# Encoder block with mixture of experts on one Trainium2 core: products moved in the tile loop, padding rows dropped from the scatter, the last expert unit taken out of the loop

## The chip, the cores and the metric

The kernel runs on one core of a Trainium2 (trn2) chip. The metric is the device time of one execution in microseconds (us). The time before is the median of 3 runs.

## What is computed

One layer over 2048 tokens of width 1024, in float32: a normalised and modulated input, a projection to q, k, v and u, windowed attention over chunks of 64 with sinks (8 query heads, 2 key heads), a pooling branch beside it, an output projection, and then a mixture of 128 experts with 8 chosen for each token, plus one shared expert.

```python
h = modulate(rmsnorm(x, norm1_g), shift1, scale1)
proj = h @ w_in                                   # q 512 | k 128 | v 128 | u 512
a = sink_window_attention(rope(q), rope(k), v, attn_sinks)
# pooling of u: band means over 2, 4, 8, 16 rows less u itself, then a 128x128 product per group
p = multiscale_pool(u, pool_w, pool_scale)
x = x + gate1 * (concat([a, p]) @ w_out)
h2 = modulate(rmsnorm(x, norm2_g), shift2, scale2)
# sigmoid router, 4 of 8 groups, 8 of 128 experts; each row of a chosen expert:
#   y = (silu(h2 @ w_gate[e]) * (h2 @ w_up[e])) @ w_down[e] * weight, added into its token's row
f = routed(h2) + swiglu(h2, w_sh_gate, w_sh_up, w_sh_down)
out = rmsnorm(x + gate2 * f, final_g)
```

2048 tokens times 8 experts are 16384 routed rows.

## The kernel before

**Order of the work.** Every engine has a queue written out by hand, with waits on named semaphores (`W8(engine, name, value)`; a wait stands in the code where the engine stops). No planner moves anything. The semaphores are named after who raises them: `p_` for TensorE, `v_` for VectorE, `a_` for ScalarE, and `B[0]` to `B[7]` are the eight PSUM banks.

**Tile loop.** The tokens go through in 16 tiles of 128 rows. `step(i)` runs on each engine for i from -2 to 17; in a step the engines work on tile i (attention and output projection), on tile i+1 (input projection), i+2 (norm), i-1 (second norm, router) and i-2 (ranks of the chosen experts, scatter of the records). On TensorE a step before the change is, in order: transposes of the next rows (L1148), scores (L1162), ranks (L1169, L1170), the input projection of the next tile (L1179, L1180, L1184), the band product of the pooling (L1191, L1192, into B[7]), transposes of h2 (L1148), transposes of the probabilities (L1200), the router product (L1211), the pool product (L1220, into B[1]), probabilities times values (L1225), transposes of the next q and k (L1233, L1234), and the output projection (L1246).

ScalarE copies PSUM banks: the projection's (L604, L605, L609, L610), the transposed h2 (L616, L617), v (L633 to L635); between them it takes the mean square of the rows of tile i+2 (L597) and then, behind a wait for VectorE's `v_v1`, its logarithm and exponential (L600, L601, each with a table load). `v_v1` is raised by `rstd_begin` on VectorE (L788), which stands behind the normalising of the probabilities (L860 to L863). VectorE also copies the band product to `mx` (L877), half of the transposed probabilities (L880) and the pool product to `mixT` (L889). `mx` shares its memory with the scratch `sq` of the mean square.

**Expert loop.** The routed rows are sorted into sub-blocks of 64 per expert, two sub-blocks make a unit of 128 rows, and there are `nu` units (158 in the trace); 158 x 128 = 20224 rows, of which 16384 are tokens and the others padding with weight 0. Weights come into a ring of four experts: SyncE issues gate and up (L388, L389) of the next expert when the ones before have landed and the slot is free, down (L394) later. A trip of the loop for unit b does on TensorE gate and up of unit b+1 (L1281, L1282), half of down of b (L1288, L1289), transposes of the rows of b+2 (L1148), transposes of the hidden rows of b+1 (L1294), and the other half of down of b. VectorE scales the result of b (L1048) and copies the gate and up weights of b+3 to a second place (L1012, 128x4096); ScalarE copies the down weights (L674). GpSimd gathers the rows of b+4 (L524, with a bounds check against the number of tokens) and adds the result of b into `acc_tab` by an indirect scatter (L558, no bounds check); padding rows go to spare rows behind each half of `acc_tab`. A scatter waits until the one before it has landed. The trip for the last unit is like all others, and works ahead on units that aren't there.

**End.** When the last scatter has landed, SyncE loads both halves of `acc_tab` (L493, L494), the halves are added (L1062), normalised (L1076) and stored (L497).

Of the kernel before, what the change touches and what calls it, by code (L numbers as in the profile page):

```python
# [6 lines left out]
P = 128  # L7
# [21 lines left out]
PAD = T  # L29
# [29 lines left out]
def constants():  # L59
# [23 lines left out]
    put("half", (s >= SUB) * (T + P))  # L83
# [27 lines left out]
def build(nc, A, out):  # L111
# [4 lines left out]
    with ctx:  # L116
# [7 lines left out]
        acc_tab = nc.dram_tensor("acc_tab", [2 * (T + P), D], f32).ap()  # L124
# [32 lines left out]
        def take(*shape):  # L157
# [72 lines left out]
        rec = sb("rec", [P, UNROLL, 2], i32)  # L230

# [9 lines left out]
            e_off e_row e_tab e_rec e_rf e_rT v_rec  # L241
# [52 lines left out]
        ys = [arena[:, 39936 + n * D:39936 + (n + 1) * D] for n in range(2)]  # L294
        hT = arena[:, 41984:42240].rearrange("p (k n) -> p k n", k=2)
# [32 lines left out]
        def _(sp):  # L328
# [93 lines left out]
            for j in range(NT):  # L422
# [9 lines left out]
                sp.dma_start(acc_tab[T + P + j * P:T + P + (j + 1) * P, :], yss[j % 2]).then_inc(s["sh_st"], 16)  # L432
# [54 lines left out]
            sp.wait_ge(s["v_cg"], nu + 3)  # L487
            settle(sp)
            sp.wait_ge(s["a_cd"], nu + 1)
            settle(sp)  # L490

            for n, (lo, hi) in enumerate(groups):
                sp.dma_start(fa[:, lo:hi, :], acc_tab[lo * P:hi * P, :].rearrange("(t p) n -> p t n", p=P)).then_inc(s[f"f_in{n}"], 16)  # L493
                sp.dma_start(fb[:, lo:hi, :], acc_tab[lo * P + T + P:hi * P + T + P, :].rearrange("(t p) n -> p t n", p=P)).then_inc(s[f"f_ib{n}"], 16)  # L494
# [7 lines left out]
        def _(g):  # L502
# [44 lines left out]
            with g.Fori(0, MAXU // UNROLL) as q:  # L547
                with g.If(q * UNROLL < nu):
# [17 lines left out]
        def _(act):  # L566
# [122 lines left out]
            with act.Fori(0, MAXU // UNROLL) as q:  # L689
                with act.If(q * UNROLL < nu):  # L690
                    for n in range(UNROLL):
                        b = act.snap(q * UNROLL + n)
                        with act.If(b < nu):
# [27 lines left out]
        def _(v):  # L721
# [93 lines left out]
            def step(i):  # L815
# [34 lines left out]
                if ok(i - 1):  # L850
# [6 lines left out]
                                    B2.rearrange("t (p k) -> t p k", k=KD), ALU.add).then_inc(s["v_h2"], 1)  # L857
                if ok(i):
# [5 lines left out]
                if ok(i + 2):  # L864
                    rstd_begin(ssq1, v1, ("a_sq1", "v_v1"), i + 3)
# [9 lines left out]
                if ok(i):  # L875
                    W8(v, "p_bd", i + 1)
                    V.tensor_copy(mx, B[7].rearrange("p (a b) -> p a b", a=4)).then_inc(s["v_mx"], 1)  # L877
                if ok(i):
# [475 lines left out]
```

## Time and profile before

| | us |
|---|---|
| median of 3 runs (2992.32 to 2997.64) | 2993.62 |
| the profiled execution | 2970.48 |
| its span, first to last instruction | 2968.5 |
| TensorE busy in the span | 2759.0 (93%) |
| VectorE, ScalarE, GpSimd busy | 1438.7, 821.8, 806.8 |

The mean granted TensorE clock is 0.971 of full speed. The profiled execution is 23.1 us shorter than the median of the runs. "Idle before" in a row is the time that the engine stood still before an instruction, with what ended it.

### The profile page before, as it was taken

Reading aid. Unit: us, or ns where it says so; the run is one execution under the profiler, and the core shown is the slowest. Engines: PE = TensorE matmul, PEld = TensorE weight load, DVE = VectorE, ACT = ScalarE, POOL = GpSimd, SP = SyncE. Lnnn points to the kernel's source line nnn. Section 1 sums busy time; section 2 is a strip of 40 time slices with the busy share of each in tenths; the row PEclk is TensorE's granted clock in tenths of the full one; section 3 lists DMA queues with packets and bytes.
Section 4 is the critical chain, followed back from the end, with each engine's and each line's share of the span. In section 5 each row is a group of like instructions: output and inputs, shape, how many; then the busy total and the mean of one; then the engine's idle time right before and its main releaser. Section 6 shows DMA issues by size and latency. Waiting matters only on the chain.

```text
span 2968.5 us, 46642 instructions
## 1 busy us (share of the span) xinstructions
PE 2759.0 (93%) x13280; PEld 1280.9 (43%) x13281; DVE 1438.7 (48%) x2384; ACT 821.8 (28%) x1265; POOL 806.8 (27%) x461
## 2 busy tenths in 40 slices
PE   5789999999889999999999999999999999999890
PEld 2366666666544433333333333333333333333330
DVE  1357777777653244444444444444444444444345
ACT  1143343334210122222222222222222222222224
POOL 0001222122211033333333323333243343343230
PEclk9899999999999999999999999999999999999995
DMA  9711121112242476789999999899989988879948
GB/s 372 233 44 57 57 71 64 57 57 71 108 176 103 159 240 210 216 277 301 310 356 348 306 357 301 267 316 331 355 268 343 305 276 259 271 228 340 360 116 345
DMA packets 150820, 684.94 MB, mean 231 GB/s; under 512 B 26434, under 2 KB 27075, under 8 KB 100867
## 3 DMA queue, kind: packets, MB, share of 16 engines
q1 hardware_dynamic: 100194, 533.08, 45.3%
q0 software_dynamic: 50592, 151.43, 22.9%
q8 instruction: 18, 0.29, 0.0%
q14 instruction: 16, 0.12, 0.0%
HBM read 574.20 MB, written 128.06 MB: 237 GB/s over the span
## 4 chain that ended last, share of the span: by engine, by line
PE 79%; DVE 7%; DMA 6%; issue 3%; ACT 3%; SPq 1%; DVEq 0%; ACTq 0%; POOLq 0%
PE PB L1281 35%; PE PB L1288 18%; PE PB L1246 8%; PE PB L1148 6%; PE PB L1102 4%; DMA arena<-in_w_up_e 3%; PE PB L1094 2%; PE PB L1125 2%; DMA arena<-in_ada_b 2%; PE PB L1211 1%; PE PB L1294 1%; DMA arena<-acc_tab 1%; DVE arena L855 1%; PE PB L1220 1%; ACT L601 1%
## 5 line engine op out<-in xcount | busy, mean ns | idle before, releaser
L1281 PE MATMUL PB<-arena 128*64 x2544 | 1118.6, 592 | 1.1 <-DVE arena L1015 1.1
L1282 PE MATMUL PB<-arena 128*64 128x512 f32 x2544 | 1118.6, 592 | 0.0
L558 POOL DMA_INDIRECT acc_tab<-arena,rec x158 | 486.6, 3080 | 1169.2 <-DVE arena L1048 987.8
L1281 PEld LDWEIGHTS PB<-arena 128*64 128x64 f32 x2544 | 348.6, 137 | 727.4 <-issue 727.4
L1289 PE MATMUL PB<-arena 128*64 128x512 f32 x1264 | 603.8, 600 | 0.0
L1288 PE MATMUL PB<-arena 128*64 x1264 | 603.7, 600 | 0.0
L1012 DVE COPY arena<-arena 128x4096 f32 x161 | 369.4, 2295 | 136.2 <-DMA arena<-in_w_up_e 65.1
L1048 DVE SCALAR_TENSOR_TENSOR arena<-PB,RW,G 128x512 f32<-128x512 f32 x316 | 222.6, 746 | 271.5 <-PE PB L1289 222.2
L1282 PEld LDWEIGHTS PB<-arena 128*64 128x64 f32 x2544 | 348.6, 137 | 0.0
L516 POOL DMA_INDIRECT rec_tab<-recs,posi x128 | 139.5, 1090 | 754.9 <-DVE recs L849 718.1
L674 ACT COPY arena<-arena 128x2048 f32 x159 | 300.5, 1890 | 0.7 <-issue 0.7
L1018 DVE TENSOR_TENSOR arena<-arena,PB 128x256 f32<-128x256 f32 x159 | 97.1, 611 | 403.7 <-ACT arena L665 403.6
L1288 PEld LDWEIGHTS PB<-arena 128*64 128x64 f32 x1264 | 160.3, 137 | 297.5 <-issue 297.5
L665 ACT ACTIVATE arena<-PB 128x256 f32<-128x256 f32 x159 | 61.0, 384 | 753.9 <-PE PB L1282 753.9
L1148 PE MATMUL PB<-cst,arena 128*128 128x128 f32 x1536 | 211.7, 282 | 34.9 <-DVE arena L885 18.2
L1148 PEld LDWEIGHTS PB<-cst,arena 128*128 128x128 f32 x1536 | 169.2, 143 | 172.7 <-issue 153.0
L1246 PE MATMUL PB<-arena 128*128 128x512 f32 x512 | 223.6, 594 | 15.8 <-ACT arena L635 15.1
L1015 DVE COPY arena<-PB 128x512 f32<-128x512 f32 x160 | 110.6, 691 | 257.8 <-PE PB L1148 257.8
L524 POOL DMA_INDIRECT arena<-h_tab,rec x162 | 169.8, 1048 | 159.5 <-issue 94.4
L668 ACT ACTIVATE arena<-PB 128x512 f32<-128x512 f32 x160 | 95.8, 599 | 372.0 <-PE PB L1148 372.0
L1289 PEld LDWEIGHTS PB<-arena 128*64 128x64 f32 x1264 | 160.4, 137 | 0.0
L1246 PEld LDWEIGHTS PB<-arena 128*128 128x128 f32 x512 | 96.0, 190 | 134.2 <-issue 133.0
(246 smaller groups left out, 2504.1 us busy)
## 6 DMA issues: line engine op xcount, KB each, us to landing
arena<-in_w_gate_e SPq DMA_DIRECT2D x128, 1024.0 KB
arena<-in_w_up_e SPq DMA_DIRECT2D x128, 1024.0 KB, 10.3
arena<-in_w_down_e SPq DMA_DIRECT2D x128, 1024.0 KB, 10.0
arena<-in_ada_w SPq DMA_DIRECT2D x12, 2048.0 KB, 13.3
arena<-in_x SPq DMA_DIRECT2D x32, 512.0 KB, 4.2
acc_tab<-arena SPq DMA_DIRECT2D x32, 512.0 KB, 3.1
arena<-acc_tab SPq DMA_DIRECT2D x6, 2048.0 KB, 22.1
h_tab<-arena SPq DMA_DIRECT2D x16, 512.0 KB, 2.9
```

What stands on the lines that cost most here:

```text
L516: g.indirect_dma_start(rec_tab, bass.IndirectOffsetOnAxis(ap=posi[:, j:j + 1], axis=0), recs[:, j, :].bitcast(i32), None).then_inc(s["st_r ...
L524: g.indirect_dma_start(xg[n % AHEAD], None, h2_tab, bass.IndirectOffsetOnAxis(ap=rec[:, n % UNROLL, 0:1], axis=0), bounds_check=T - 1, oob ...
L558: g.indirect_dma_start(acc_tab, bass.IndirectOffsetOnAxis(ap=rec[:, n, 1:2], axis=0), ys[n % 2], None, compute_op=ALU.add).then_inc(s["add ...
L674: nc.scalar.copy(WBD, RING[:, bass.ds(act.snap(at + GUW), HALF)]).then_inc(s["a_cd"], 1)
L1012: V.tensor_copy(WBGf[n % 2], RING[:, bass.ds(at, GUW)]).then_inc(s["v_cg"], 1)
L1048: last_ = V.scalar_tensor_tensor(out=ys[n % 2][:, c * 512:(c + 1) * 512], in0=B[4 + c], scalar=RW[:, bass.ds(b, 1)], in1=G2[:, c * 512:(c ...
L1148: last = tr(B[banks[k // 4]][:, (k % 4) * P:(k % 4 + 1) * P], src[:, k * P:(k + 1) * P], ident)
L1246: last = mm(B[4 + n], mixT[:, k, :], w_out[:, k, n * 512:(n + 1) * 512], start=(k == 4), stop=(k == 3))
L1281: mm(B[7][0:SUB, :], xTm[:, k, 0:SUB], wa(k), start=(k == 0), stop=(k == KD - 1))
L1282: last = mm(B[7][SUB:P, :], xTm[:, k, SUB:P], WBG[n % 2][:, k], start=(k == 0), stop=(k == KD - 1))
L1288: mm(B[4 + c][0:SUB, :], hT[:, k, 0:SUB], wa(k), start=(k == 0), stop=(k == 1))
L1289: last = mm(B[4 + c][SUB:P, :], hT[:, k, SUB:P], WBD[:, k * D + c * 512:k * D + (c + 1) * 512], start=(k == 0), stop=(k == 1))
```

## The change

Band product of tile i: behind the scores, ahead of the ranks and the input projection. Pool product: behind the transposes of the probabilities, ahead of the router product, and into bank 7 and not 1; its wait for the probabilities' copies goes. VectorE: `rstd_begin` for the next rows ahead of the normalising of the probabilities; copy of the band product ahead of the rope; copy of the pool product ahead of the end of the norm. The output projection waits for the attention's copy only at its fifth product, and for v's only at its second half. Expert loop: padding rows get an index past the table and are dropped by a bounds check; the spare rows of `acc_tab` and their zeroing shrink; the loop runs to nu - 1 and the last unit has code of its own behind it (down product, scale, scatter) with buffers of its own.

```diff
-PAD = T
+PAD = 2 * T + P
...
-    put("half", (s >= SUB) * (T + P))
+    put("half", (s >= SUB) * T)
...
-        acc_tab = nc.dram_tensor("acc_tab", [2 * (T + P), D], f32).ap()
+        acc_tab = nc.dram_tensor("acc_tab", [2 * T + P, D], f32).ap()
...
-            sp.wait_ge(s["v_cg"], nu + 3)
+            sp.wait_ge(s["v_cg"], nu + 2)
...
-            sp.wait_ge(s["a_cd"], nu + 1)
+            sp.wait_ge(s["a_cd"], nu)
...
             for n in range(2):
-                at = T + n * (T + P)
-                g.dma_start(acc_tab[at:at + P, :], zeros).then_inc(s["added"], 16)
+                at = 2 * T + n * SUB
+                g.dma_start(acc_tab[at:at + SUB, :], zeros[0:SUB, :]).then_inc(s["added"], 16)
...
-                        with g.If(b < nu):
+                        with g.If(b + 1 < nu):
...
-                                                 ys[n % 2], None, compute_op=ALU.add).then_inc(s["added"], 16)
+                                                 ys[n % 2], None, bounds_check=2 * T - 1, oob_is_err=False, compute_op=ALU.add).then_inc(s["added"], 16)
                     settle(g)
+            g.wait_ge(s["y_v"], nu + 1)
+            g.wait_ge(s["v_rec_last"], 1)
+            g.wait_ge(s["added"], nu * 16 + 16)
+            settle(g)
+            g.indirect_dma_start(acc_tab, bass.IndirectOffsetOnAxis(ap=rec_last[:, 1:2], axis=0),
+                                 ys_last, None, bounds_check=2 * T - 1, oob_is_err=False, compute_op=ALU.add).then_inc(s["added"], 16)
```

VectorE in a step, and behind the loop:

```diff
+                if ok(i + 2):
+                    rstd_begin(ssq1, v1, ("a_sq1", "v_v1"), i + 3)
                 if ok(i):
                     W8(v, "a_exp", i + 1)
...
                     V.tensor_tensor(sc, sc, sinv.unsqueeze(2).to_broadcast([P, NH, P]), ALU.mult).then_inc(s["v_P"], 1)
-                if ok(i + 2):
-                    rstd_begin(ssq1, v1, ("a_sq1", "v_v1"), i + 3)
+                if ok(i):
+                    W8(v, "p_bd", i + 1)
+                    V.tensor_copy(mx, B[7].rearrange("p (a b) -> p a b", a=4)).then_inc(s["v_mx"], 1)
...
+            V.tensor_copy(rec_last[:, :], pair[:, bass.ds(nu - 1, 1), :].rearrange("p n a -> p (n a)")).then_inc(s["v_rec_last"], 1)
+            v.wait_ge(s["y_done"], nu)
+            settle(v)
+            for c in range(2):
+                last_ = V.scalar_tensor_tensor(out=ys_last[:, c * 512:(c + 1) * 512], in0=B[4 + c], scalar=RW[:, bass.ds(nu - 1, 1)],
+                                               in1=G2[:, c * 512:(c + 1) * 512], op0=ALU.mult, op1=ALU.mult)
```

TensorE in a step, and behind the loop:

```diff
+                if ok(i):
+                    W8(pe, "a_u", i + 1)
...
+                    last.then_inc(s["p_bd"], 1)
                 if ok(i - 2):
...
+                    W8(pe, "v_mx", i + 1)
+                    W8(pe, "c_wt", 80)
+                    for g_ in range(NPG):
+                        last = mm(B[7][:, g_ * P:(g_ + 1) * P], poolw[:, g_, :], mx[:, g_, :], start=True, stop=True)
+                    last.then_inc(s["p_py"], 1)
...
                     for n in range(2):
+                        if n == 1 and ok(i + 1):
+                            W8(pe, "a_v", i + 2)
                         for k in (4, 5, 6, 7, 0, 1, 2, 3):
+                            if n == 0 and k == 0:
+                                W8(pe, "a_aT", i + 1)
...
+            pe.wait_ge(s["y_v"], nu)
+            pe.wait_ge(s["hT_a"], nu)
+            pe.wait_ge(s["a_cd"], nu)
+            down(0, down_a(0))
+            down(1, down_a(1)).then_inc(s["y_done"], 1)
```

**On TensorE, end of a step of the tile loop.** Before, from the transposes of h2 (L1148) and of the probabilities (L1200) on: router, pool product, values, next q and k, output projection.

```order
L1148 MATMUL PB<-cst,arena 128x128 [waits v_h2]
L1200 MATMUL PB<-cst,arena 128x128 [waits v_P]
L1211 MATMUL PB<-arena 128x128 [waits a_u,v_rank,c_rest,a_h2T]
L1220 MATMUL PB<-arena,poolw 128x128 [waits a_v,v_PT,v_mx,c_wt,a_PT]
L1225 MATMUL PB<-arena 64x4x64 x4
L1233 MATMUL PB<-cst,arena 128x128 [waits a_u,a_rt,v_rope]
L1234 MATMUL PB<-cst,arena 128x128
L1246 MATMUL PB<-arena 128x512 [waits a_u,a_v,a_qk,v_fold,v_yT,a_aT]
```

Now:

```order
L1164 MATMUL PB<-cst,arena 128x128 [waits v_h2]
L1216 MATMUL PB<-cst,arena 128x128 [waits v_P]
L1221 MATMUL PB<-arena,poolw 128x128 [waits c_wt,v_mx]
L1232 MATMUL PB<-arena 128x128 [waits a_u,v_rank,c_rest,a_h2T]
L1241 MATMUL PB<-arena 64x4x64 [waits a_v,v_PT,a_PT]
L1251 MATMUL PB<-cst,arena 128x128 [waits a_rt,a_u,v_yT,v_rope]
L1252 MATMUL PB<-cst,arena 128x128
L1266 MATMUL PB<-arena 128x512 [waits a_u,v_fold,a_qk,v_yT]
L1266 MATMUL PB<-arena 128x512 [waits a_aT]
L1266 MATMUL PB<-arena 128x512 [waits a_v]
```

The pool product stands ahead of the router product and waits for `v_mx` alone of the tile's copies; the transposes of the next q and k wait for `v_yT` too; the waits of the output projection are spread over three of its products.

**On VectorE, between h2 (L856, now L864) and the rope (L871, now L882).** Before:

```order
L856 TENSOR_TENSOR arena<-arena 128x128x8 [waits v_ch]
L860 TENSOR_REDUCE smallc<-arena 128x8 [waits a_exp]
L863 TENSOR_TENSOR arena<-arena,smallc 128x1024 [waits v_ch]
L788 TENSOR_SCALAR smallc<-smallc 128x1 [waits a_sq1]
L871 ISA [waits a_trig,a_qk]
```

Now:

```order
L864 TENSOR_TENSOR arena<-arena 128x128x8 [waits v_ch]
L796 TENSOR_SCALAR smallc<-smallc 128x1 [waits a_sq1]
L870 TENSOR_REDUCE smallc<-arena 128x8 [waits a_exp]
L873 TENSOR_TENSOR arena<-arena,smallc 128x1024 [waits v_ch]
L876 COPY arena<-PB 128x512 [waits p_bd]
L882 ISA [waits a_trig,a_qk]
```

The small instruction that releases ScalarE (L788, now L796) stands ahead of the three that normalise the probabilities, and the copy of the band product ahead of the rope's wait for the projection's copies.

## Rows read from the trace of the kernel before

**Rows 1.** Windows, expert loop: us, then busy us (count) by engine, granted clock, DMA share, GB/s.

```profile
1500.00:2000.00 500.00, 499.93 (x2482) 190.05 (x2480) 215.84 (x257) 135.46 (x172) 171.28 (x86) 1.00 0.95 323
```

**Rows 2.** Waits of TensorE to 1060 us: us in total, times, longest.

```profile
PE PB L1211 <- ACT arena L617: 28.6, 14, 2.4
...
PE PB L1246 <- ACT arena L635: 15.1, 15, 1.0
```

**Rows 3.** Timeline of one step: start us, us, engine, line, operation [idle before].

```profile
468.41 2.03 DVE L856 TENSOR_TENSOR arena<-arena 128x1024 f32<-128x1024 f32 x1
...
471.91 0.39 PE L1191 MATMUL PB<-cst,arena 128*128 128x128 f32 x2
...
473.09 0.15 DVE L788 TENSOR_SCALAR smallc<-smallc 128x1 f32<-128x1 f32 x1
...
473.70 1.04 PE L1148 MATMUL PB<-cst,arena 128*128 128x128 f32 x8
...
474.89 0.58 ACT L604 ACTIVATE arena<-PB 128x512 f32<-128x512 f32 x1
...
477.21 0.62 ACT L617 ACTIVATE arena<-PB 128x512 f32<-128x512 f32 x1
...
477.88 2.05 PE L1211 MATMUL PB<-arena 128*128 128x128 f32 x16 [2.27 <-ACT arena L617]
...
479.77 1.06 PE L1220 MATMUL PB<-arena,poolw 128*128 128x128 f32 x8
...
483.55 0.67 PE L1246 MATMUL PB<-arena 128*128 128x512 f32 x1 [1.00 <-ACT arena L635]
```

**Rows 4.** Chain of waits, starts of three output projections: start us, us, what.

```profile
312.77 13.97 PE PB L1246 x32
...
356.27 13.97 PE PB L1246 x32
...
398.15 13.97 PE PB L1246 x32
```

**Rows 5.** Windows within one step, columns as in rows 1.

```profile
435.00:438.50 3.50, 3.50 (x19) 3.50 (x18) 2.60 (x3) 0.28 (x1) 0.00 (x0) 0.51 0.37 150
```

**Rows 6.** Timeline of the last two units.

```profile
2875.70 1.89 ACT L674 COPY arena<-arena 128x2048 f32 x1
...
2878.06 3.34 POOL L558 DMA_INDIRECT acc_tab<-arena,rec  x1 [7.02 <-DVE arena L1048]
...
2887.41 1.41 DVE L1048 SCALAR_TENSOR_TENSOR arena<-PB,RW,G 128x512 f32<-128x512 f32 x2 [1.70 <-PE PB L1289]
...
2889.37 2.29 DVE L1012 COPY arena<-arena 128x4096 f32 x1 [0.47 <-issue]
...
2889.75 3.37 POOL L558 DMA_INDIRECT acc_tab<-arena,rec  x1 [7.01 <-DVE arena L1048]
```

**Rows 7.** Chain of waits, landing of the last scatter.

```profile
2889.75 7.50 DMA acc_tab<-arena,rec
```

**Rows 8.** DMA issues of the whole execution: count, median us to landing.

```profile
acc_tab<-arena,rec POOLq DMA_INDIRECT x158, 8.6
```

**Rows 9.** GpSimd in the timeline, a scatter and a gather while VectorE waits.

```profile
2784.05 1.58 POOL L558 DMA_INDIRECT acc_tab<-arena,rec  x1 [8.77 <-DVE arena L1048]
...
2785.93 1.04 POOL L524 DMA_INDIRECT arena<-h_tab,rec  x1 [0.30 <-issue]
```

**Rows 10.** Timeline, TensorE and VectorE at the one stall of the expert loop.

```profile
2811.82 0.69 PE L1294 MATMUL PB<-cst,arena 128*128 128x128 f32 x2 [9.16 <-DVE arena L1018]
...
2808.97 2.29 DVE L1012 COPY arena<-arena 128x4096 f32 x1 [14.08 <-DMA arena<-in_w_up_e]
```

**Rows 11.** SyncE's queue, first and last of the six loads before it.

```profile
2740.46 0.35 SPq L388 DMA_DIRECT2D arena<-in_w_gate_e  x1
...
2797.94 0.34 SPq L388 DMA_DIRECT2D arena<-in_w_gate_e  x1
```

**Rows 12.** DMA queues from 2887 to 2898 us, the last scatter alone.

```profile
q0 software_dynamic: 144, 0.52, 28.5%
```

More of the change, by code:

```diff
@@ L689, in _ @@
             with act.Fori(0, MAXU // UNROLL) as q:
-                with act.If(q * UNROLL < nu):
+                with act.If(q * UNROLL + 1 < nu):
                     for n in range(UNROLL):
                         b = act.snap(q * UNROLL + n)
-                        with act.If(b < nu):
+                        with act.If(b + 1 < nu):
                             at = act.value_load(tab[0:1, bass.ds(b + (2 * P + 1), 1)], min_val=0, max_val=(SLOTS - 1) * EW)
@@ L1035, in _ @@
             with v.Fori(0, MAXU // UNROLL) as q:
-                with v.If(q * UNROLL < nu):
+                with v.If(q * UNROLL + 1 < nu):
                     for n in range(UNROLL):
                         b = v.snap(q * UNROLL + n)
-                        with v.If(b < nu):
+                        with v.If(b + 1 < nu):
                             v.wait_ge(s["eg_done"], b + 2)
@@ L1164, in step @@
                     last.then_inc(s["p_sc"], 1)
+                if ok(i):
+                    W8(pe, "a_u", i + 1)
+                    bd = C("band0") if isinstance(i, int) and i == 0 else C("band")
+                    for g_ in range(NPG):
+                        cs = slice(g_ * P, (g_ + 1) * P)
+                        mm(B[7][:, cs], uC[:, cs], bd[:, cs], start=True, stop=False)
+                        last = mm(B[7][:, cs], uP[:, cs], C("bandp")[:, cs], start=False, stop=True)
+                    last.then_inc(s["p_bd"], 1)
                 if ok(i - 2):
@@ L1185, in step @@
                     last.then_inc(s["p_proj"], 1)
-                if ok(i):
-                    W8(pe, "a_u", i + 1)
-                    bd = C("band0") if isinstance(i, int) and i == 0 else C("band")
-                    for g_ in range(NPG):
-                        cs = slice(g_ * P, (g_ + 1) * P)
-                        mm(B[7][:, cs], uC[:, cs], bd[:, cs], start=True, stop=False)
-                        last = mm(B[7][:, cs], uP[:, cs], C("bandp")[:, cs], start=False, stop=True)
-                    last.then_inc(s["p_bd"], 1)
                 if ok(i - 1):
@@ L1201, in step @@
                     last.then_inc(s["p_PT"], 1)
+                    W8(pe, "v_mx", i + 1)
+                    W8(pe, "c_wt", 80)
+                    for g_ in range(NPG):
+                        last = mm(B[7][:, g_ * P:(g_ + 1) * P], poolw[:, g_, :], mx[:, g_, :], start=True, stop=True)
+                    last.then_inc(s["p_py"], 1)
                 if ok(i - 1):
@@ L1214, in step @@
                     W8(pe, "a_PT", i + 1)
-                    W8(pe, "c_wt", 80)
                     W8(pe, "v_PT", i + 1)
                     W8(pe, "a_v", i + 1)
-                    W8(pe, "v_mx", i + 1)
-                    for g_ in range(NPG):
-                        last = mm(B[1][:, g_ * P:(g_ + 1) * P], poolw[:, g_, :], mx[:, g_, :], start=True, stop=True)
-                    last.then_inc(s["p_py"], 1)
                     O = B[0].rearrange("p (a b) -> p a b", a=4)
@@ L1229, in step @@
                     W8(pe, "v_rope", i + 2)
+                    if ok(i):
+                        W8(pe, "v_yT", i + 1)
                     W8(pe, "a_rt", i)
@@ L1307, in _ @@
             with pe.Fori(0, MAXU // UNROLL) as q:
-                with pe.If(q * UNROLL < nu):
+                with pe.If(q * UNROLL + 1 < nu):
                     for n in range(UNROLL):
                         b = pe.snap(q * UNROLL + n)
-                        with pe.If(b < nu):
+                        with pe.If(b + 1 < nu):
                             at1 = pe.value_load(tab[0:1, bass.ds(b + 1, 1)], min_val=0, max_val=(SLOTS - 1) * EW)
```

28 lines of the change are left out of this document (15 added, 13 removed).

## The prediction

> **What bounds the kernel now.** I read the windows by stage first, then the waits of TensorE, then the timeline of one step of the tile loop, then the ends of both loops. In the expert loop TensorE is busy 499.93 of 500 us while the DMA engines stand at 0.95 [rows 1]: that stage lasts as long as its matmuls, 11.69 us for a unit (the two scatters of [rows 6] are that far apart), and only an edit that takes matmuls out, or a wait that TensorE really has, can shorten it. In the tile loop TensorE is the last engine too, but it stands still twice in a step: 28.6 us in all ahead of the router product, for ScalarE's copy of the transposed h2, and 15.1 us ahead of the output projection, for ScalarE's copy of v [rows 2]. Whatever takes these away is gained in full as long as no other engine needs the time. VectorE is the next busiest, with 1438.7 us of the span against 2759.0.
>
> **Band product, and the mean square sooner.** In the step shown the projection's last matmul is issued by 471.91, where the band product starts; that lasts until 473.70 [rows 3], 1.8 us. Moved ahead of the projection it costs the same 1.8 us there, and the projection ends at 473.7 in place of 471.9: nothing on TensorE, and h2's transposes (473.70) stay where they are. ScalarE's first copy of the projection starts only at 474.89, though: ScalarE is held by its logarithm and exponential, which wait for L788 on VectorE at 473.09, so 1.8 us after that instruction ScalarE is free [rows 3]. With L788 directly behind h2 (L856 ends at 470.44) ScalarE is free at 472.3, and then waits for the projection, about 473.9. All its copies come 1.0 us sooner, the last of h2 ends at 476.8 and not 477.83, and the router product can start at 476.9 in place of 477.88. VectorE's small instruction delays the probabilities by 0.15 us; they are finished at about 473.3, and their transposes start behind those of h2, after 474.5, so that is covered. If that cover were gone, each tenth would cost a tenth a step.
>
> **Pool product.** TensorE falls idle at 475.6 (477.88 less 2.27). The pool product now stands in that gap; it takes 0.9 us (the row at 479.77 lasts 1.06 with its pipeline). It needs the copy of the band product, which VectorE can now make straight behind the probabilities, by 474.0. Idle left: 476.9 - 475.6 - 0.9 = 0.4 us, where 2.27 stood. I carry 0.4 for the 12 full steps. Its bank 7 has to be empty before the next q and k are transposed, so a new wait (`v_yT`) stands ahead of them; VectorE's rope, its copy of the probabilities and this copy are done by about 477.3, the transposes start near 480, slack 2.7 us. Late next would be these copies.
>
> **Output projection.** Its wait of 1.0 us [rows 3] was for the last copy of v. It now asks for the attention's copy after four of its eight products of the first half (3.5 us in) and for v's after the first half (7 us in), while these copies end within 2 us. I cost the wait at 0.
>
> Sum in the tile loop: 28.6 + 15.1 - 12 x 0.4 = 38.9 us. Bounds: 26.9 if ScalarE's copies come no sooner (1.4 us stay idle in 12 steps), 43.7 if nothing stays.
>
> **The clock.** Starts of output projections are 43.50 and 41.88 us apart [rows 4]; of the 14 distances six are the long one. In each long one the granted clock falls to the lower of its two levels, 1.2 GHz, for 3.4 us (0.51 in the stretch of [rows 5]), just behind the gap of some 2.3 us, never behind a gap of 1.0. With the gap at 0.4 I expect none: 6 x 1.62 = 9.7 us. From below 0: they stay. I take 9.7, since only the long gap goes with them.
>
> The Trainium skill (TensorE: Matmul & The Clock Gate, "A second HAM failure mode: psum-queue depth-cycling") says that short idles between groups of matmuls, often enough, make the clock oscillate. By it the falls stay and the sum is 9.7 us smaller; no row shows a fall behind the short gap alone.
>
> **The loop one unit shorter.** TensorE loses one gate and up that nobody needs. The last unit's down must now wait for ScalarE's weight copy, L674, to 2877.6 on the clock of the trace [rows 6]; it is 8 of a unit's 24 pairs of products, so at most 3.9 us, and ends by 2881.6 and is scaled (1.41 us) by 2883.2, where the scaling ended at 2888.8 [rows 6]. But the last scatter also waits for the one before, issued at 2878.06 [rows 6] and, if it takes 7.50 us as the last does [rows 7], landed at 2885.6. So this landing, not TensorE, sets the end. Issue comes 0.9 us behind the release (2888.82 to 2889.75), at 2886.5. The descriptors took 3.37 us on GpSimd beside VectorE's 2.29 us copy L1012 [rows 6]; that copy is not made then any more, and where VectorE was waiting the same instruction took 1.58 us [rows 9]. Landing: 2886.5 + 7.50 - 1.8 = 2892.2 against 2897.25: 5.0 us. From below 3 (no shorter descriptors, the empty trips of the loop in the way), from above 6.5. The new code on the other engines lies beside that landing.
>
> The Trainium skill (SBUF — State Buffer, the "DVE blocks DMA" trap) gives 0.62 us alone and 3.1 us overlapped for such a DMA's descriptors. By it this saves 2.5 us and not 1.8, and the sum is 0.7 larger; the rows show 1.58, which I use.
>
> **Dropped rows.** 158 scatters [rows 8] carry 20224 rows, of which 16384 are tokens: 19% go. The loop is TensorE's but for one place, 9.16 us near its end, where VectorE waits 14.08 us for a weight load [rows 10]; six loads, each begun when the one before had landed, lead up to it [rows 11]. One scatter alone keeps the 16 engines busy for 28.5% of 11 us [rows 12], 3.1 us; 19% of that is 0.6, six times 3.6 us. From below 0 (the engines handle dropped rows as before), from above 12.5, all of the stall and its slow clock. The smaller zeroing at the start lies beside the first weight strips: 0. What the check costs GpSimd no row shows for a scatter; the gather, with such a check, takes 1.04 us [rows 9]. Each unit has room: 11.69 - 8.6 [rows 8] - 0.9 = 2.2 us.
>
> **Sum**: 38.9 + 9.7 + 5.0 + 3.6 = 57.2 us. Against the profiled execution, 2970.5, that is 2913.3; against the median of the runs, 2993.6, it is **2936.4**. The profiled one was 23.1 us faster than that median for no reason that it can show; if longer stalls for weights are it, dropped rows bring more, up to 8 us by the same share.
>
> **Rivals.**
> - *The clock still falls* (12%). The short idles go on and six falls stay: 2936.4 + 9.7 = 2946.1. Against: falls only at the long gap.
> - *ScalarE's copies come no sooner* (8%). 1.4 us of the gap stays and with it the falls: 26.9 + 5.0 + 3.6 = 35.5, 2958. For: ScalarE has six copies in a row there. Against: 1.8 us from L788 to the first copy.
> - *The whole stall goes* (15%). 12.5 in place of 3.6: 2927.5. For: a queue that only just falls behind catches up.
> - *Dropped rows cost the same* (4%): 2936.4 + 3.6 = 2940.
> - *Slower: the scatter becomes the bound* (3%). A scatter waits for the landing of the last. If the check lengthens each by more than 2.2 us, the rest is paid 158 times; with 2.6 us more the gain is gone (158 x 0.36 = 57), with 3.0 us the time is 2936.4 + 158 x 0.8 = 3063. Against: the gather's 1.04 us.
> - My forecast itself: 58%.
>
> **How the numbers follow.** Smallest gain that I hold likely: the 35.5 of the second rival, 2958; since only part of its chance is wanted, 2957. Largest: 43.7 + 9.7 + 6.5 + 12.5, with 5 more where the timed runs stall longer: 77.4, 2916. The range 2916 to 2957 leaves out the slower rival and half of the second. A change of 0.2% (6 us) is what a measurement can tell: faster 0.96, same 0.01, slower 0.03.
>
> **What would show it.** Right: distances of output projections near 39.1 us, all alike, no granted clock of 0.5 between 200 and 750 us; wait ahead of the router product about 0.4 us, none ahead of the output projection; last scatter under 2 us on GpSimd, issued 0.9 us behind the landing of the one before; stall in the expert loop near 5.5 us. Wrong: a wait of TensorE for `v_yT` or for the probabilities' copies, or scatters over 11 us apart from each other's landing.

## The result, and the profile after

The changed kernel takes 2913.57 us (median of 4 runs, 2912.57 to 2920.7) where the kernel before takes 2995.35 (4 runs, 2992.32 to 2997.64) beside it: ratio 0.9729 [0.9714, 0.9744], 81.8 us faster. Forecast were 57.2 us, 2936.4 with a range from 2916. The sign is right; the gain is 25 us larger, and the time lies 2.4 us below the range.

The profiled executions tell another story: 2970.5 before, 2912.6 after, 57.9 us apart. Before's profile was 23 to 25 us quicker than its timed runs, and 2970.48 is none of them; after's is 1 us quicker than the median of its own, and is one of them. The page of the changed kernel, for [rows 8] and the totals:

```profile
span 2910.5 us, 46033 instructions
...
PE 2740.6 (94%) x13238; PEld 1269.5 (44%) x13239; DVE 1437.1 (49%) x2381; ACT 821.0 (28%) x1261; POOL 801.7 (28%) x460
...
q0 software_dynamic: 50320, 135.21, 21.0%
...
L560 POOL DMA_INDIRECT acc_tab<-arena,rec x157 | 478.7, 3049 | 1162.1 <-DVE rec L1059 815.2
```

TensorE is busy 18 us less (2759.0 to 2740.6), which includes products that ran under the lower clock; the rest of the 58 us was idle time. GpSimd's own DMA queue moves 135.21 MB and not 151.43, and a scatter takes 3049 ns on GpSimd where it took 3080, in the page of before:

```profile
q0 software_dynamic: 50592, 151.43, 22.9%
...
L558 POOL DMA_INDIRECT acc_tab<-arena,rec x158 | 486.6, 3080 | 1169.2 <-DVE arena L1048 987.8
```

The waits of TensorE in the whole span, for [rows 2]:

```profile
PE PB L1232 <- ACT arena L625: 9.7, 14, 0.8
PE PB L1314 <- DVE arena L1026: 4.1, 4, 3.2
PE PB L1308 <- ACT arena L682: 2.7, 1, 2.7
PE PB L1241 <- ACT arena L628: 1.8, 6, 0.8
```

The 28.6 us ahead of the router product have become 9.7 (expected: 0.4 a step), and the 15.1 us ahead of the output projection are gone. The windows of the tile loop, before and then after (core and columns as in [rows 1]):

```profile
200.00:840.00 640.00, 585.48 (x3162) 415.73 (x3160) 464.24 (x1119) 236.41 (x477) 123.02 (x112) 0.98 0.20 69
```

```profile
200.00:752.00 552.00, 539.61 (x3017) 388.60 (x3016) 438.32 (x1053) 225.61 (x457) 115.44 (x104) 1.00 0.22 72
```

The granted clock is 1.00 from 200 to 752 us, and the chain shows output projections at nearly even distances (39.5, 39.6, 39.3, 39.5 us) in place of the 43.50 and 41.88 of [rows 4]:

```profile
262.19 13.74 PE PB L1266 x32
...
301.71 13.73 PE PB L1266 x32
...
341.26 13.74 PE PB L1266 x32
...
380.51 13.74 PE PB L1266 x32
...
420.02 13.73 PE PB L1266 x32
```

The idle ahead of the router product is 0.7 to 0.8 us in most steps here. The timeline of a step, for [rows 3]:

```profile
413.01 0.60 ACT L612 ACTIVATE arena<-PB 128x512 f32<-128x512 f32 x1 [2.17 <-PE PB L1208]
...
413.28 1.04 PE L1216 MATMUL PB<-cst,arena 128*128 128x128 f32 x8
...
416.02 2.05 PE L1232 MATMUL PB<-arena 128*128 128x128 f32 x16 [0.81 <-ACT arena L625]
417.44 0.60 ACT L628 ACTIVATE arena<-PB 128x512 f32<-128x512 f32 x1 [1.48 <-remote]
417.44 0.69 DVE L888 COPY arena<-PB 128x512 f32<-128x512 f32 x1 [2.53 <-remote]
...
419.86 1.02 PE L1266 MATMUL PB<-arena 128*128 128x512 f32 x2
```

ScalarE is free 2.17 us before L612 and waits for the projection: it is no longer what is late. But the transposes of the probabilities (L1216) end at 414.32, and their two copies on ScalarE and VectorE start together only at 417.44, 3.1 us later. Both wait for the same semaphore, the one that those transposes raise, and neither engine has other work in that time (the profile writes `remote`, as it finds no releaser). So in this execution a signal of TensorE came later than the modelled end of its products.

The end, the timeline's rows for [rows 6], and the chain's for [rows 7]:

```profile
2823.47 1.89 ACT L682 COPY arena<-arena 128x2048 f32 x1
...
2825.90 3.29 POOL L560 DMA_INDIRECT acc_tab<-arena,rec  x1 [7.07 <-DVE arena L1056]
...
2834.68 1.56 POOL L567 DMA_INDIRECT acc_tab<-arena,rec_last  x1 [5.49 <-DMA acc_tab<-arena,rec]
```

```profile
2825.90 7.88 DMA acc_tab<-arena,rec
2834.68 4.45 DMA acc_tab<-arena,rec_last
```

The last scatter waits for the landing of the one before (5.49 us of idle end with that DMA), starts 0.9 us behind it, and takes 1.56 us on GpSimd. The end goes as the forecast drew it, with a shorter last landing.

The time of each stage, from the starts of the first and the last output projection and of the first and the last scatter in each profile (us):

| profile | to the first output projection | tile loop | between | expert loop | end | span |
|---|---|---|---|---|---|---|
| before | 188.6 | 629.4 | 223.5 | 1848.3 | 78.7 | 2968.5 |
| changed | 183.4 | 587.6 | 222.6 | 1841.0 | 75.8 | 2910.5 |
| changed, third profile, where before takes 2973 | 182.8 | 580.5 | 222.6 | 1844.7 | 76.0 | 2906.7 |

The tile loop gives 41.8 and 48.9 us (forecast: 48.6). What was left open was why the medians are 24 us further apart (81.8) than the two profiled executions (57.9).

### The profile page after: what moved, and what is told of

Same layout as the page of the kernel before. It is cut to its first block, busy times and chain, and to the rows that moved or that the text cites. A ratio compares the mean times of both kernels' runs of the same rounds, so it can differ in the third digit from the quotient of the medians.

```text
span 2910.5 us, 46033 instructions
## 1 busy us (share of the span) xinstructions
PE 2740.6 (94%) x13238; PEld 1269.5 (44%) x13239; DVE 1437.1 (49%) x2381; ACT 821.0 (28%) x1261; POOL 801.7 (28%) x460
## 3 DMA queue, kind: packets, MB, share of 16 engines
q0 software_dynamic: 50320, 135.21, 21.0%
## 4 chain that ended last, share of the span: by engine, by line
PE 87%; DMA 6%; DVE 3%; ACT 2%; issue 1%; SPq 1%; another core or an unknown queue 0%; DVEq 0%; ACTq 0%; POOLq 0%
PE PB L1301 35%; PE PB L1308 18%; PE PB L1266 8%; PE PB L1164 6%; PE PB L1118 4%; DMA arena<-in_w_up_e 3%; PE PB L1208 3%; PE PB L1203 2%; PE PB L1204 2%; PE PB L1110 2%; PE PB L1141 2%; DMA arena<-in_ada_b 2%; PE PB L1314 1%; PE PB L1178 1%; DMA arena<-acc_tab 1%
## 5 line engine op out<-in xcount | busy, mean ns | idle before, releaser
L560 POOL DMA_INDIRECT acc_tab<-arena,rec x157 | 478.7, 3049 | 1162.1 <-DVE rec L1059 815.2
L1308 PE MATMUL PB<-arena 128*64 x1264 | 605.3, 601 | 2.7 <-ACT arena L682 2.7
L682 ACT COPY arena<-arena 128x2048 f32 x158 | 298.6, 1890 | 0.7 <-issue 0.7
L1308 PEld LDWEIGHTS PB<-arena 128*64 128x64 f32 x1264 | 160.7, 137 | 302.5 <-issue 302.5
```

The lines of the kernel that those rows point to most:

```text
L560: g.indirect_dma_start(acc_tab, bass.IndirectOffsetOnAxis(ap=rec[:, n, 1:2], axis=0), ys[n % 2], None, bounds_check=2 * T - 1, oob_is_err= ...
L682: nc.scalar.copy(WBD, RING[:, bass.ds(act.snap(at + GUW), HALF)]).then_inc(s["a_cd"], 1)
L1308: mm(B[4 + c][0:SUB, :], hT[:, k, 0:SUB], wa(k), start=(k == 0), stop=(k == 1))
```

## The experiments

Two theories of the missing 25 us. The one: the terms were too small, and some part of the change brings more than its profile shows. The other: the terms are right, and the kernel *before* loses more than in its profile in some places where it runs. The expectations split them further and give them letters: the loss is stalls for weights in the expert loop (A), more falls of the clock in the tile loop (B), or a profile is always shorter than the timed runs (C); the terms are right and before was high on that chip (P), the parts bring more together than alone (Q); something comes late in each step, which lengthens the gap and brings more falls (R). A fall is a stretch in which the granted clock goes from 2.4 to 1.2 GHz; the gap is TensorE's idle time ahead of the router product. The first runs take the change apart; the later ones take the tile loop's part apart, repeat both kernels on other chips, and imitate a loss. All ratios are to the kernel before on the same chip. Gains without another word are differences of medians.

**Before, once more.** Edit: none.

> The kernel before, unchanged, to see its timed executions' spans and its profile again. The question is the 23 us by which its first profiled execution (2970.5) was shorter than the median of its runs (2995). Theory A (stalls for weights in the expert loop): a profile at about 2993 shows 2 to 4 waits of TensorE in the expert loop with 30 us in all where the first showed one of 9.2, and the same distances of output projections (six of 43.5). Theory B (clock): the profile shows the lower clock behind nearly every long gap, 14 falls and not 6, 13 us more, and the expert loop as before. Theory C: a profile is always shorter by 23 us than a timed run: the profile shows 2970 again while the runs show 2993.

Measured: 2975.73 beside 2976.37 (27 runs, 2970.7 to 2981.41), 0.9998 [0.9989, 1.0008]. The same kernel is 20 us quicker here than in the first comparison, and within 5 us of its first profile; its profile and its runs agree, so theory C falls. 18 to 20 of the 23 to 25 us belong to where or when it ran. On this chip theories A and B have nothing to explain.

**The tile loop's part alone.** Edit: all hunks of the tile loop, none of the expert loop.

> The reordered tile loop alone, with the expert loop and scatter of before. By my terms 38.9 + 9.7 = 48.6 us less, 2947 against 2995. Theory A (the missing 24 us are stalls for weights, which the dropped rows cure): 2947, no more. Theory B (in timed runs before has up to 14 falls of the clock in the tile loop, all cured): 38.9 + 23 = 62 us less, 2933.

Measured: 2923.06 (4 runs), 0.9822 [0.9807, 0.9837]: 53.3 us, where the sum had 48.6. Idle ahead of the router product is 0.40 us in all but two steps (0.60 and 0.69), the projections are mostly 38.9 us apart, and the clock does not fall between 200 and 740 us.

**Dropped rows alone.**

```diff
-PAD = T
+PAD = 2 * T + P
...
-                                                 ys[n % 2], None, compute_op=ALU.add)
+                                                 ys[n % 2], None, bounds_check=2 * T - 1, oob_is_err=False, compute_op=ALU.add)
```

> The dropped padding rows alone (bounds check, smaller table), all else of before. Theory A: 24 + 3.6 = about 28 us less, 2967. Theory B: 3.6 us less, 2991. If the check made scatters longer: more than 2995.

Measured: 2971.5 (11 runs), 0.9991 [0.9979, 1.0003]: 2.7 us by the ratio, 4.9 by the medians, for a forecast of 3.6. The stall in the expert loop is 10.8 us here, no shorter than the 9.16 of [rows 10]. What is shorter is the landing of the last scatter, for which all else waits:

```profile
2891.73 6.34 DMA acc_tab<-arena,rec
```

It took 7.50 us in [rows 7] and 7.84 to 8.20 in the five later profiles of before; beside the new tile loop (a later run) it is 6.36 in place of 7.85 and 7.92.

**The shorter loop alone**, padding rows still written. Edit: the loop's `if b < nu` becomes `if b + 1 < nu`, with the code behind it.

> The loop one unit shorter alone, padding rows still written to spare rows. My term: 5.0 us less, 2990, under both theories. Theory D (the last unit's code outside the loop takes away more at the end, such as a slow fetch of the loop's last trips): over 15 us less.

Measured: 2970.77 (11 runs), 0.9981 [0.9972, 0.999]: 5.6 us, forecast 5.0.

**The changed kernel again, on another chip.** Edit: none.

> The changed kernel, unchanged. Theory P (the terms are right, and the runs of before that it was first compared with stood 20 us high on that chip): its gain over before on the chip of these runs is 53 (tile loop, as measured alone) + 5.6 (shorter loop) + 2.7 to 4.9 (dropped rows) = 61 to 64 us, 2913 if before is again 2976. Theory Q (the parts bring more together than alone): over 75 us, under 2900. Its profile should show whether the idle time ahead of the router product is again 0.78 us a step, as in its first profile, where the tile loop alone has 0.40.

Measured: 2912.22 beside 2989.97 (9 runs, 2986.18 to 2997.5), 0.9748 [0.9731, 0.9765]: 77.8 us. The gain is what theory Q named (over 75), the time is what theory P named (2913, not under 2900): before is high here too, and the changed kernel is not. Before's runs have a mean granted clock of 0.968 to 0.970 here, where most on the chip of the four runs above show 0.971 to 0.972. The gap ahead of the router product is 0.72 to 0.78 us in 11 of 14 steps, as in the profile after.

**Pairs of parts, same chip as the last.** Edits: the tile loop's part with the dropped rows; the tile loop's part with the shorter loop.

> Tile loop and dropped rows, without the shorter loop. Theory P: 56 to 58 us less than before. Theory Q: over 65. If the 0.4 us more a step of the changed kernel come with the dropped rows, the idle time ahead of the router product is 0.78 here; if they come with the code of the shorter loop, 0.40.

> Tile loop and the loop one unit shorter, padding rows still written. Theory P: 53 + 5.6 = 59 us less than before. Theory Q: over 65. Idle ahead of the router product 0.78 if the longer code of the shorter loop does it, 0.40 if not.

Measured: 2924.65, 0.9779 [0.9764, 0.9793], and 2919.69, 0.9768 [0.9753, 0.9782]: 65.3 and 70.3 us. Both hold the tile loop's part, which gave 53.3 us on the other chip. If the small parts are worth here what they are worth alone (2.7 to 4.9, and 5.6), 60 to 65 us are left for the tile loop's part, 7 to 11 more than there. That they are is not shown: the whole change is 12.4 and 7.5 us quicker than the pairs, more than 5.6 and 4.9 (by the ratios 9.3 and 6.0, which with these intervals is not told from them), and the tile loop's part was not run alone on this chip. What falls is that the dropped rows cure the extra loss (theory A): the pair without them gains 70.3. Their tile loops take 587.6 and 587.8 us, as the changed kernel's 587.5 here, against 581.9 for the tile loop's part on the other chip: the new loop is not quicker here, so it is *before* that is slower. The gap of 0.7 to 0.8 us stands in both pairs, so neither the dropped rows nor the shorter loop's code brings it.

**Before, a third chip.**

> The kernel before once more, for a profile on a chip where it runs at 2990 and not at 2976 (its median was 2995 and 2990 on two chips, 2976 on a third). Theory R: on such a chip ScalarE starts an instruction some 0.4 to 1.5 us late in each step of the loop (in the changed kernel its first copy of the projection starts 0.4 us behind the projection, 0.04 in the tile loop's first run), which lengthens the gap ahead of the router product to about 2.7 us and lets the clock fall in 10 or more steps and not in 6: 0.4 x 12 + 5 x 1.6 = 13 us more, a mean clock of 0.969. Theory A (stalls for weights): the tile loop as in the first profile, 15 us more of waits in the expert loop. If this chip has 2976, the profile is as in the first.

Measured: 2974.17 beside 2973.15, 1.0004. This is no chip on which before takes 2990, so theories A and R were not tested. Gap 2.25 us, seven clock falls, tile loop 632.3. Waits of TensorE to 1060 us:

```profile
PE PB L1211 <- ACT arena L617: 28.4, 14, 2.3
```

**The mean square late again.** In the tile loop's part, `rstd_begin` goes back behind the normalising of the probabilities:

```diff
-                if ok(i + 2):
-                    rstd_begin(ssq1, v1, ("a_sq1", "v_v1"), i + 3)
                 if ok(i):
                     W8(v, "a_exp", i + 1)
...
+                if ok(i + 2):
+                    rstd_begin(ssq1, v1, ("a_sq1", "v_v1"), i + 3)
                 if ok(i):
                     W8(v, "p_bd", i + 1)
```

> The reordered tile loop, but the small instruction for the mean square stays behind the normalising of the probabilities (ahead of the copy of the band product). Expected: ScalarE free 1.8 us after it again, idle ahead of the router product 1.4 us in place of 0.4 to 0.8, so 8 to 12 us more than the tile loop alone (2923 where before is 2976). If the clock falls at gaps of 1.4 us it is up to 10 us more still; if only at gaps over 2, none.

Measured: 2930.43, 0.9854 [0.9838, 0.9871]: 42.7 us, 10.6 less than the whole part.

```profile
PE PB L1216 <- ACT arena L617: 16.1, 14, 1.4
```

The gap is 1.25 to 1.35 us in 12 steps, 0.87 more than 0.40, together 10.5 us: the loss is this gap alone, and the clock does not fall. The prediction's second rival was that the copies come no sooner, which leaves 1.4 us idle and the falls with it. The first half is imitated here; the second does not follow, since 1.25 to 1.35 us of idle bring no fall.

**Only the mean square sooner**, in the kernel before; bands, pool and waits as they were.

```diff
+                if ok(i + 2):
+                    rstd_begin(ssq1, v1, ("a_sq1", "v_v1"), i + 3)
                 if ok(i):
                     W8(v, "a_exp", i + 1)
...
-                if ok(i + 2):
-                    rstd_begin(ssq1, v1, ("a_sq1", "v_v1"), i + 3)
```

> Only the small instruction for the mean square sooner, all else of before. ScalarE is free at the projection's end, but its copy of the pooled rows then waits for the band product behind the projection. Expected idle ahead of the router product 0.7 to 1.2 us in place of 2.27, the 1.0 us ahead of the output projection as before, no falls of the clock: 1.3 x 12 + 9.7 = 25 us less than before. A rival says that the copy's wait gives nothing back: 0 to 5 us less.

Measured: 2942.08, 0.9898 [0.9881, 0.9914]: 31.1 us by moving one instruction of VectorE, where 25 were expected.

```profile
PE PB L1246 <- ACT arena L635: 15.1, 15, 1.0
PE PB L1211 <- ACT arena L617: 9.0, 14, 0.6
```

28.6 - 9.0 = 19.6 us of idle and, with no falls left, 9.7 of clock: 29.3. Without this move, the moved band and pool products bring the gap from 2.25 to 1.27 us (the run above); on top of it, they bring it from 0.64 to 0.40.

**The output projection's old waits**, in the tile loop's part:

```diff
                 if ok(i):
+                    W8(pe, "a_aT", i + 1)
...
+                        W8(pe, "a_v", i + 2)
...
-                        if n == 1 and ok(i + 1):
-                            W8(pe, "a_v", i + 2)
```

> The reordered tile loop, but the output projection waits at its start for the attention's copy and for v's, as before. Expected: 1.0 us idle ahead of each output projection again, 15 us more than the tile loop alone, and no falls of the clock, since gaps of 1.0 us never brought one.

Measured: 2939.74, 0.9881 [0.9864, 0.9898]: 33.4 us, 20 less than the part with the new waits by the medians, 18 by the ratios; 15 were expected.

```profile
PE PB L1248 <- ACT arena L635: 15.1, 15, 1.0
PE PB L1216 <- ACT arena L617: 5.6, 14, 0.4
```

All of the wait was real, and a little more: starts of output projections are 40.12 us apart in place of 38.88, which is 1.24 us a step for a wait of 1.00, and the 32 products behind the wait take 13.97 us in place of 13.74 (13.97 is also what [rows 4] show). The chain of this run:

```profile
387.18 13.97 PE PB L1248 x32
...
427.29 13.97 PE PB L1248 x32
```

The clock does not fall with a gap of 1.00 us.

**Both kernels again.** Edits: none (before, on the chip of the first runs of this section); the tile loop's part; before on another chip; the changed kernel there; before once more.

> The kernel before, for its profile where it runs at 2990. Theory R (late starts of ScalarE in each step, seen in the changed kernel on one chip): gap ahead of the router product 2.6 us or more, 10 or more falls of the clock in the tile loop, mean clock 0.969. Theory A (stalls for weights in the expert loop): tile loop unchanged, 15 us more waits there. If the median is again 2976, nothing is told, and the gap is 2.27 with seven falls.

> The reordered tile loop alone. Theory R: where before takes 2990 it gains about 67 us (53 and the 14 more of before), where before takes 2976 it gains 53. Theory A: it gains 53 on either, 2937 where before takes 2990.

> The kernel before, for its profile where it runs at 2990. Theory R: gap ahead of the router product 2.6 us or more and 10 or more falls of the clock, mean clock 0.969. Theory A: tile loop unchanged, 15 us more waits in the expert loop. With a median of 2973 nothing is told of this.

> The changed kernel. Where before takes 2973, theory P says 61 us less, 2912, and 4 us less than that if its idle time ahead of the router product is 0.4 and not 0.78 there. Where before takes 2990, 2912 again, 78 less.

> The kernel before. Theory R, on a chip where it takes 2990: gap ahead of the router product 2.6 us or more, 10 or more falls of the clock, mean clock 0.969. Theory A: tile loop unchanged, 15 us more waits in the expert loop. With 2973 nothing is told.

Measured: 2972.23 beside 2973.06, five falls; 2919.25, 0.9821 [0.9804, 0.9837], 53.8 us; 2973.45 beside 2972.54, seven falls; 2908.55, 0.9787 [0.9766, 0.9808], **64.0 us**; 2973.24 beside 2973.36. So on a chip where before takes 2973 the whole change brings 64, where 65 were expected (61, and 4 with a gap of 0.4 us), and on none of these chips did before take more than 2974: no place where before takes 2990 was met again, so its profile there is missing, and theories A and R were not tested by one. The changed kernel's waits there, and the distances of its output projections (38.88 us):

```profile
PE PB L1232 <- ACT arena L625: 5.6, 14, 0.4
```

```profile
260.58 13.74 PE PB L1266 x32
...
299.46 13.74 PE PB L1266 x32
...
338.34 13.74 PE PB L1266 x32
```

This is the forecast's picture: 0.4 us in each step, and 38.9 where 39.1 was forecast. The 4 us that the profile after has more (9.7 against 5.6) stand only in the profiles with the late signals.

**A delay imitated.** If something late on ScalarE's path lengthens the gap of before and brings more falls, a delay put there must do the same; the changed kernel, in which ScalarE waits 2.17 us for the projection, must hide it.

```diff
-ACT_PER_TILE = 7
+ACT_PER_TILE = 9
...
                     ch.link(A_(l1, v1, ACT.Ln))
+                    for _ in range(2):
+                        ch.link(A_(y1, l1, ACT.Exp, scale=-0.5))
                     A_(y1, l1, ACT.Exp, scale=-0.5).then_inc(s["a_y1"], 1)
```

> The kernel before with ScalarE held 0.45 us longer ahead of its copies in each step (the exponential of the mean square made three times over, each behind the last), to copy the late starts seen on one chip. Theory R: the gap ahead of the router product grows from 2.25 to 2.7 us (13 steps, 5 to 6 us) and the lower clock comes in most steps and not in every second (4 to 6 falls more, 1.6 us each): 13 to 16 us more than before, 2988. Rival: only the gap grows, 5 to 6 us, 2979.

> The changed kernel with the same 0.45 us on ScalarE. There ScalarE is free 1.8 us ahead of the projection's end, so the extra work is covered: 0 us more, 2909 where before takes 2973, and no fall of the clock. If ScalarE's reserve were less than I think, up to 6 us more.

Measured in before: 2983.44 beside 2973.53 (9 runs), 9.9 us slower by the medians and 8.6 [4.8, 12.5] by the ratio of 1.0029, between theory R (13 to 16) and its rival (5 to 6); in the changed kernel 2911.05, 0.9785 [0.9767, 0.9802]. The waits of TensorE in before with the delay (200 to 800 us) and its window; then the same stretch of before:

```profile
PE PB L1213 <- ACT arena L619: 34.6, 14, 2.7
```

```profile
200.00:800.00 600.00, 551.24 (x3000) 398.67 (x2999) 435.65 (x1050) 228.19 (x482) 114.60 (x104) 0.97 0.20 66
```

```profile
200.00:800.00 600.00, 556.42 (x3064) 399.53 (x3062) 439.64 (x1058) 225.34 (x459) 113.37 (x104) 0.98 0.20 67
```

The gap grows by 0.5 us, to 2.71 to 2.74 (6.0 us in all, 34.6 for 28.6), and 9 falls stand where 5 to 7 stood, at 1.62 us each; the tile loop takes 641.7 us in place of 628.6 to 632.3. The mean clock of five of the six runs is 0.969 to 0.970, near that of the chip on which before takes 2990. In the changed kernel the gap stays at 0.40, the clock does not fall between 200 and 740 us, and the tile loop takes 580.6 us (580.5 without the delay):

```profile
PE PB L1234 <- ACT arena L627: 5.6, 14, 0.4
```

So a small delay costs before more than itself, and the changed kernel nothing that can be measured. That is the kind of loss that could fill the 14 to 20 us; this one fills 9 to 10. What would be late there is not known.

## Why the prediction was wrong in size

**The step that failed** is the last one, behind the sum: "against the median of the runs, 2993.6, it is 2936.4. The profiled one was 23.1 us faster than that median for no reason that it can show". The terms were subtracted from the higher of the two times as if its 23 us would stay. They did not: the kernel before takes 2972 to 2976 us on four chips and 2990 to 2995 in two comparisons, while the changed kernel takes 2909 to 2914 wherever it ran. Of the 24.6 us by which the gain was missed, 18 to 20 are this offset; the other 5 to 7 are terms of the sum, below. Against the profiled execution the sum gave 2913.3; measured were 2912.6 in the profile and 2913.6 in the median, and that this fits so closely is in part luck, as the last paragraph of this section shows. The prediction looked for the 23 us in longer stalls for weights, which dropped rows would shorten. The runs speak against it: the pair that still writes the padding rows gains 70.3 us where before takes 2990, and in the profiles there the stall is short (2.9 us in the changed kernel, 2.8 and 4.8 in the pairs).

What the 14 to 20 us are is not settled. For longer gaps and more clock falls in the tile loop: the mean clock of before is lower there, the imitated delay gives nearly the same mean clock, and the changed kernel does not feel it. Against a full proof: the imitation costs 9 to 10 us and not 14 to 20, a mean clock does not say in which stage it fell, the tile loop's part was not run alone there, and no profile of before was caught where it takes 2990, so its gap there was never read. Nor do the late signals explain it as they were seen. In before, ScalarE's first copy of the projection starts 2.8 us behind the projection, held by its logarithm and exponential [rows 3], so a signal that comes 0.4 us late is covered. And three profiles on a chip where before takes 2973 to 2976 (before again, dropped rows alone, shorter loop alone) have the copies of the probabilities 3.0 us late too, with a gap of 2.25 us in all steps but one (2.8 us there) and 6 or 7 falls.

Term by term, where before takes 2972 to 2976:

- *Tile loop's idle, 38.9 us.* Right. Ahead of the router product 5.6 us stay of 28.6 (4.8 forecast); ahead of the output projection none of 15.1. The late mean square put back costs 10.6 us. The old waits put back cost 18 to 20 and not 15.1, since the products behind them are 0.23 us quicker without them; the forecast had no term for this.
- *Band product sooner, at no cost.* Right: ScalarE waits for the projection (2.17 us ahead of L612) and nothing waits for the band product.
- *Pool product in the gap, and the wait for `v_yT`.* Right. That wait shows on L1251 only twice between 200 and 752 us:

```profile
PE PB L1251 <- DVE arena L892: 1.7, 2, 1.0
```

- *The clock, 9.7 us.* Right in kind: in the tile loop no falls with gaps of 0.4, 0.64, 0.78, 1.0 and 1.27 us, five to seven with 2.25, nine with 2.73. The term is 1.62 us for each fall, and before's falls are not the same number in each execution. By the Trainium skill (TensorE: Matmul & The Clock Gate, "A second HAM failure mode: psum-queue depth-cycling"), frequent short idles between groups of products make the clock oscillate, and the falls would have stayed, as in the first rival. This did not come true: 14 short idles, one every 39 us, leave the clock at 2.4 GHz.
- *Both together 48.6 us*: measured 53.3 and 53.8 (53.0 and 53.2 by the ratios). 48.9 is what the tile loop itself gives in the table; the stage ahead of the first output projection, which the sum left out, gives most of the rest: 186.7 to 189.7 us in the profiles of before, 183.7 to 186.7 in four with the tile loop's part alone or nearly so, 182.4 to 184.8 in four of the changed kernel. Dropped rows alone have 185.2, so the ranges lie close to each other.
- *The end, 5.0 us*: 5.6 alone. The landing ahead took 7.88 us and not 7.50. The last one took 4.45 and not 5.7; it is 6.23 in the shorter loop alone, so the rest comes with the dropped rows. The descriptors' 1.56 us without VectorE's copy beside them agree with [rows 9]. TensorE's wait for the last weight copy, 2.7 us (L1308 for L682), is where the forecast put it, and beside the landing as forecast.
- *Dropped rows, 3.6 us*: 2.7 [-0.9, 6.2]. The size is hardly resolved, and the place was wrong. The term was priced as a shorter stall, and no profile shows that dropped rows shorten it; what they shorten is the landing of the last scatter, 6.34 us for 7.50 to 8.20, for which the sum had nothing. The stall is 2.8 to 11.6 us long from profile to profile, with dropped rows or without: 9.2 to 10.2 before, 8.1 and 11.6 with the tile loop's part alone, 10.8 with the dropped rows alone, 2.9 to 10.5 in the changed kernel. In the profile after it is this pair:

```profile
2756.72 2.29 DVE L1020 COPY arena<-arena 128x4096 f32 x1 [8.14 <-DMA arena<-in_w_up_e]
...
2759.57 0.69 PE L1314 MATMUL PB<-cst,arena 128*128 128x128 f32 x2 [3.23 <-DVE arena L1026]
```

VectorE still waits 8.14 us for a weight load, TensorE 3.23. In the changed kernel with the imitated delay, on another chip, TensorE waits 10.5. A stall that differs by 8 us between profiles cannot be priced from one of them.
- *The bounds check.* Free, as far as this shows: 3049 ns for a scatter on GpSimd where 3080 stood; the traffic that goes is 151.43 - 135.21 = 16.2 MB. The slower rival falls with it.

Where before takes 2973, the sum is 57.2, with some 4 us for the first stage 61, and 64.0 are measured (57 to 70 by the ratio's interval). That the two profiled executions are 57.9 us apart, so near to 57.2, is in part luck: after's tile loop was 7 us longer than in the third profile (587.6 against 580.5), its expert loop 3.7 us shorter.

## What to carry to other kernels

Where a profiled execution and the median of the same kernel differ by more than the spread, ask whether both were taken in the same place, and whether the change removes the difference too; put both cases into the range instead of carrying the offset along. An idle gap on the critical engine is also a place where small delays around it are paid (the imitated delay cost 9 to 10 us with the gap, nothing without it), so closing it can give more than its measured length. And a stall that has another length in each profile of the same kernel is worth a range, not a share.

## What was unexpected of the hardware

- The same kernel takes 2972 to 2976 us on four chips and 2990 to 2995 in two other comparisons, the changed one 2909 to 2914 in all: how much the place matters depends on the kernel.
- The signal of a finished group of products can come late. In the profiles of the changed kernel (first and second) and of the two pairs, ScalarE's first copy of the input projection starts 0.4 us after the products' modelled end in most steps, and the copies of the probabilities' transposes 1.6 to 3.1 us after it; in the third profile of the changed kernel it is 0.03 us, and 0.1 for VectorE's copy. With it the tile loop is 7 us longer (587.6 against 580.5). It is not bound to a chip: the 3.0 us stand in three profiles of the chip of the first runs and not in the later ones there. The cause is open.
- In the first two profiles of the changed kernel and those of the two pairs, the expert loop is 3 to 13 us shorter than in the others of the new tile loop (1841.0 to 1841.8 against 1844.7 to 1854.4), so the two loops' times partly cancel. Why is open.
- The clock's fall comes in some steps with the same 2.25 us of idle and not in others, 5 to 7 times in some 14 steps, but 9 times with 2.73 us.
- The same 32 products of the output projection take 13.97 us behind a wait and 13.74 us without one.
